# Expert outputs summed in memory by accumulating indirect DMA, instead of by rank and on VectorE at the end

## What is computed

```
idx, w = top-8 experts of 64 for each token, with weights
routed[t] = sum over the 8 experts e of token t:  w[t,e] * swiglu(h[t], w_gate[e], w_up[e], w_down[e])
shared[t] = swiglu(h[t], w_sh_gate, w_sh_up, w_sh_down)
f = routed + shared
y = x1 + g2 * rms_norm(f) * norm_post_ffn
```

## Time and profile before

| | |
|---|---|
| median of three runs | 1228.45 us (1228.25 to 1231.38) |
| the profiled execution, its own time | 1229.39 us |
| span of that execution (first to last instruction) | 1227.6 us |
| busy: PE, DVE, ACT, POOL | 1108.3, 902.1, 638.6, 186.9 us |
| mean granted TensorE clock | 0.944 of full speed |
| scatters, first and last issue | 545.1 and 1168.3 us |

### The profile page before, as it was taken

One profiled execution on the slowest core, in us unless ns is written; L12 is line 12 of the kernel. 1 busy time (PEld: TensorE's weight loads), 2 busy tenths in 40 slices (PEclk: granted clock), 3 DMA queues, 4 the chain that ended last, 5 costly groups with the idle time before them and its releaser, 6 DMA issues.

```text
span 1227.6 us, 18502 instructions
## 1 busy us (share of the span) xinstructions
PE 1108.3 (90%) x6006; PEld 804.5 (66%) x6006; DVE 902.1 (73%) x1306; ACT 638.6 (52%) x765; POOL 186.9 (15%) x185
## 2 busy tenths in 40 slices
PE   5899999999989989899999999999999999999700
PEld 0699999966444454467777777777777777777400
DVE  0732444267866776688899999988998888898878
ACT  1432222232421132357788777777777777777401
POOL 0200000000110010122222222222222222221102
PEclk8699999999879999999999999999999999999855
DMA  9532221163975124599999999999999999998996
GB/s 369 180 94 93 78 78 65 57 193 103 369 264 191 43 80 178 192 327 386 391 391 383 388 383 387 384 384 385 380 380 376 377 380 379 378 381 310 350 351 216
DMA packets 87140, 339.86 MB, mean 277 GB/s; under 512 B 12515, under 2 KB 36083, under 8 KB 59204
## 3 DMA queue, kind: packets, MB, share of 16 engines
q1 hardware_dynamic: 70724, 301.68, 66.6%
q0 software_dynamic: 16384, 37.78, 8.8%
HBM read 317.52 MB, written 42.86 MB: 294 GB/s over the span
## 4 chain that ended last, share of the span: by engine, by line
PE 41%; DMA 37%; DVE 14%; ACT 6%; issue 2%; SPq 1%; DVEq 0%; POOL 0%; POOLq 0%; ACTq 0%
DMA arena<-in_w_exp_down 31%; PE ps L1787 12%; DVE down_lo L1617 5%; PE ps L2023 4%; ACT down_hi L1102 4%; DMA arena<-in_w_ada 3%; PE ps L2215 3%; PE ps L2194 2%; PE ps L1780 2%; PE ps L2195 2%; PE ps L2196 2%; PE ps L2061 1%; DMA arena<-expert_rows 1%; PE ps L2198 1%; DMA arena<-in_w_in 1%
## 5 line engine op out<-in xcount | busy, mean ns | idle before, releaser
L1622 DVE TENSOR_TENSOR gu_lo<-w_gu,gu_hi 128x2048 fp32r<-128x2048 f32 (+1 forms) x128 | 258.5, 2020 | 6.0 <-ACT gu_hi L1096 1.1
L1096 ACT ACTIVATE gu_hi<-w_gu 128x2048 fp32r<-128x2048 f32 (+1 forms) x128 | 217.9, 1703 | 0.0
L1617 DVE TENSOR_TENSOR down_lo<-arena,down_hi 128x2048 fp32r<-128x2048 f32 x64 | 146.7, 2292 | 60.2 <-ACT down_hi L1102 60.2
L2194 PE MATMUL ps<-gu_hi,xT_hi 128*112 128x512 f32 x448 | 181.5, 405 | 3.7 <-DVE xT_lo L1627 2.6
L2195 PE MATMUL ps<-gu_lo,xT_hi 128*112 128x512 f32 x448 | 176.5, 394 | 0.0
L2196 PE MATMUL ps<-gu_hi,xT_lo 128*112 128x512 f32 x448 | 176.1, 393 | 0.0
L1102 ACT ACTIVATE down_hi<-arena 128x2048 fp32r<-128x2048 f32 x64 | 122.7, 1917 | 68.8 <-DMA arena<-in_w_exp_down 64.4
L811 POOL DMA_INDIRECT expert_rows<-arena,row_idx x64 | 69.8, 1091 | 360.7 <-ACT arena L1141 345.3
L1787 PE MATMUL ps<-w_hi,hT_hi 128*128 128x300 f32 x384 | 116.4, 303 | 2.0 <-DVE w_lo L1185 2.0
L1787 PE MATMUL ps<-w_lo,hT_hi 128*128 128x300 f32 x384 | 115.9, 302 | 0.0
L1787 PE MATMUL ps<-w_hi,hT_lo 128*128 128x300 f32 x384 | 115.7, 301 | 0.0
(11 more groups left out here) (297 smaller groups left out, 1891.5 us busy)
## 6 DMA issues: line engine op xcount, KB each, us to landing
w_gu<-in_w_exp_gate SPq DMA_DIRECT2D x64, 1024.0 KB
w_gu<-in_w_exp_up SPq DMA_DIRECT2D x64, 1024.0 KB
arena<-in_w_exp_down SPq DMA_DIRECT2D x64, 1024.0 KB
arena<-in_w_ada SPq DMA_DIRECT2D x24, 1024.0 KB, 8.8
arena<-in_w_in SPq DMA_DIRECT2D x12, 1200.0 KB, 5.6
arena<-expert_rows SPq DMA_DIRECT2D x9, 1024.0 KB, 13.8
arena<-expert_rows SPq DMA_DIRECT2D x4, 2048.0 KB, 13.0
arena<-in_x_prompt SPq DMA_DIRECT2D x8, 512.0 KB, 9.3
```

The costliest lines, as they stand in the source:

```text
L1096: a.activation(gu_hi[b % RING][:, :, ks], w_gu[b % U][:, :, ks], ACT.Copy).then_inc(s_ghi, 1)
L1617: v.tensor_tensor(down_lo[:, :, :], w_dn[b % RING], down_hi[:, :, :].bitcast(F32), ALU.subtract).then_inc(s_dlo, 1)
L1622: v.tensor_tensor(gu_lo[b % U][:, :, ks], w_gu[b % U][:, :, ks], gu_hi[b % RING][:, :, ks].bitcast(F32), ALU.subtract).then_inc(s_glo, 1)
L2194: pe.matmul(out, x_hi, gu_hi[r][:, :, k], start=(k == 0), stop=False)
```

## The change

`expert_rows` has one row for each token instead of eight, and begins as the shared expert's output: SP stores `shared` to it where it stored it to `kept_rows` before. Each scatter adds its rows to what is there (`compute_op=ALU.add`), and goes to the token's row. POOL waits, ahead of the first scatter, until that store is done. The other scatters wait for the one before them, as they did. At the end the summed rows are read back once, 4 KiB for each token, all five tiles behind the last scatter (`s_tick`); `x1` is loaded ahead of that, once the last block's gate and up matmuls are done. `low_ranks`, `middle_ranks` and `high_ranks` are gone, and with them `s_add` and the rank loads.

```diff
             def scatter(j, b):
                 g.wait_ge(s_ya, j + 2)
                 g.sem_inc(s_pulse, 1)
                 g.indirect_dma_start(expert_rows[:, :], bass.IndirectOffsetOnAxis(row_idx[0:T, b:b + 1].bitcast(U32), 0),
-                                     y_rows[0:T, b % 2], None, bounds_check=last_scatter,
-                                     oob_is_err=False).then_inc(s_ys[b], 16)
+                                     y_rows[0:T, b % 2], None, bounds_check=last_gather,
+                                     oob_is_err=False, compute_op=ALU.add).then_inc(s_ys[b], 16)
...
                     elif not is_first:
                         g.wait_ge(s_ys[U - 1], 16 * i)
+                    else:
+                        g.wait_ge(s_mst, 32 + 64)
...
-            for rows, buf in kept(N, shared):
-                sp.dma_start(rows, buf).then_inc(s_mst, 16)
+            sp.dma_start(expert_rows[0:SEQ, :].rearrange("(t p) d -> p t d", p=P), shared[:, 0:PT]).then_inc(s_mst, 16)
+            sp.dma_start(expert_rows[SEQ:N, :], shared[0:NS, PT]).then_inc(s_mst, 16)
...
             load_down(last * U + RING, RING, True)
-            sp.wait_ge(s_free, last * U + 2)
-            for t in range(2):
-                sp.wait_ge(s_gu, last * U + (t + 1))
-                rank_rows(ranks_low[t], 0, 4, t)
             load_down(last * U + 3, 3, True)
-            for t in range(2, NT):
-                ...
-                rank_rows(ranks_low[t], 0, 4, t)
             sp.wait_ge(s_gu, last * U + 4)
-            for rows, buf in kept(N, shared):
-                sp.dma_start(buf, rows).then_inc(s_bcg, 16)
-            sp.wait_ge(s_free, last * U + 4)
-            sp.wait_ge(s_dlo, last * U + 3)
+            for rows, buf in kept:
+                sp.dma_start(buf, rows).then_inc(s_fx, 16)
+            sp.wait_ge(s_tick, 1)
             for t in LAST_ORDER:
-                sp.wait_ge(s_add, (5, 4, 3, 4, 5)[t])
-                rank_rows(ranks_mid[t], 4, 2, t)
-            sp.wait_ge(s_y, last * U + U)
-            sp.wait_ge(s_tick, 1)
-            for n, t in enumerate(LAST_ORDER):
-                sp.wait_ge(s_add, NT + n + 1)
-                rank_rows(ranks_high[t], 6, 2, t)
-                ...
+                sp.dma_start(shared[0:ROWS[t], t], expert_rows[t * P:t * P + ROWS[t], :]).then_inc(s_yb[t], 16)
...
-                a.wait_ge(s_add, 2 * NT + n + 1)
-                a.activation(sq2[0:R], ranks_high[t][0:R, 0], ACT.Square, accum_out=ss[0:R, 3, t:t + 1]).then_inc(s_q3, 1)
+                a.wait_ge(s_yb[t], 16)
+                a.activation(sq2[0:R], shared[0:R, t], ACT.Square, accum_out=ss[0:R, 3, t:t + 1]).then_inc(s_q3, 1)
...
-                v.scalar_tensor_tensor(out=row_idx[0:T, b:b + 1], in0=slot_info_kept[0:T, bass.ds(at + 2, 1)], scalar=float(N),
-                                       in1=token_idx[0:T, b:b + 1], op0=ALU.mult, op1=ALU.add).then_inc(s_wt, 1)
+                v.tensor_copy(row_idx[0:T, b:b + 1], token_idx[0:T, b:b + 1]).then_inc(s_wt, 1)
...
             for n, t in enumerate(LAST_ORDER):
-                middle_ranks(t, NT + n + 1)
-            high_ranks(0, LAST_ORDER[0])
-            for n, t in enumerate(LAST_ORDER):
-                if n + 1 < NT:
-                    high_ranks(n + 1, LAST_ORDER[n + 1])
                 normalised(n, t)
```

More of the change, by code:

```diff
@@ L346, in hybrid_step @@
         slot_w = sb("slot_w", [P, U])
[L348 to L352, removed]
         sq2 = region(WORK0 + 8 * D, D)
@@ L493, in hybrid_step @@
         s_rowtile = sem("row_tile_changed")
-        s_yb = [sem(f"rank_rows_in{t}") for t in range(NT)]
-        s_add = sem("combined")
+        s_yb = [sem(f"summed_rows_in{t}") for t in range(NT)]
         s_q3 = sem("ffn_square_sum")
@@ L670, in _ @@
                 store_h2(t)
-            def kept(first, buf):
-                yield kept_rows[first:first + SEQ, :].rearrange("(t p) d -> p t d", p=P), buf[:, 0:PT]
-                yield kept_rows[first + SEQ:first + N, :], buf[0:NS, PT]
+            kept = ((kept_rows[0:SEQ, :].rearrange("(t p) d -> p t d", p=P), x1[:, 0:PT]), (kept_rows[SEQ:N, :], x1[0:NS, PT]))
             def load_gate_up(j, b, wait):
@@ L694, in load_down @@
                 sp.dma_start(w_dn[b % RING], down).then_inc(s_wdn[b % RING], 16)
-            for rows, buf in kept(0, x1):
+            for rows, buf in kept:
                 sp.dma_start(rows, buf).then_inc(s_mst, 16)
@@ L721, in _ @@
                     load_down(i * U + (b + RING), (b + RING) % U, True)
-            by_rank = expert_rows.rearrange("(k n) d -> n k d", n=N)
-            def rank_rows(to, first, k, t):
-                sp.dma_start(to[0:ROWS[t], 0:k], by_rank[t * P:t * P + ROWS[t], first:first + k]).then_inc(s_yb[t], 16)
             load_down(last * U + RING, RING, True)
-            sp.wait_ge(s_free, last * U + 2)
-            for t in range(2):
-                sp.wait_ge(s_gu, last * U + (t + 1))
-                rank_rows(ranks_low[t], 0, 4, t)
             load_down(last * U + 3, 3, True)
-            for t in range(2, NT):
[L734 to L737, removed]
-                rank_rows(ranks_low[t], 0, 4, t)
             sp.wait_ge(s_gu, last * U + 4)
-            for rows, buf in kept(N, shared):
-                sp.dma_start(buf, rows).then_inc(s_bcg, 16)
-            sp.wait_ge(s_free, last * U + 4)
-            sp.wait_ge(s_dlo, last * U + 3)
+            for rows, buf in kept:
+                sp.dma_start(buf, rows).then_inc(s_fx, 16)
+            sp.wait_ge(s_tick, 1)
             for t in LAST_ORDER:
-                sp.wait_ge(s_add, (5, 4, 3, 4, 5)[t])
-                rank_rows(ranks_mid[t], 4, 2, t)
-            sp.wait_ge(s_y, last * U + U)
-            sp.wait_ge(s_tick, 1)
-            for n, t in enumerate(LAST_ORDER):
-                sp.wait_ge(s_add, NT + n + 1)
-                rank_rows(ranks_high[t], 6, 2, t)
-                if n == 1:
-                    for rows, buf in kept(0, x1):
-                        sp.dma_start(buf, rows).then_inc(s_fx, 16)
+                sp.dma_start(shared[0:ROWS[t], t], expert_rows[t * P:t * P + ROWS[t], :]).then_inc(s_yb[t], 16)
             for n, t in enumerate(LAST_ORDER):
                 sp.wait_ge(s_fin, n + 1)
-                sp.dma_start(tok_rows(y_prompt, y_sample, t), ranks_high[t][0:ROWS[t], 1]).then_inc(s_out, 16)
+                sp.dma_start(tok_rows(y_prompt, y_sample, t), shared[0:ROWS[t], t]).then_inc(s_out, 16)
             sp.wait_ge(s_out, 16 * (3 * H + NT))
@@ L796, in _ @@
             last_gather = g.to_reg(N - 1)
-            last_scatter = g.to_reg(N * TOPK - 1)
             def gather(j, b, wait=True):
@@ L1671, in turn @@
                         gate_up_low(i * U + (b + 3), b + 3, 0)
[L1672 to L1693, removed]
             def normalised(n, t):
-                R, y = ROWS[t], ranks_high[t][0:ROWS[t]]
+                R, y = ROWS[t], shared[0:ROWS[t], t]
                 v.wait_ge(s_r3, n + 1)
-                step(v.scalar_tensor_tensor(out=y[:, 1], in0=y[:, 0], scalar=rstd[0:R, 3, t:t + 1], in1=bcg2[t // PT][0:R],
+                step(v.scalar_tensor_tensor(out=y, in0=y, scalar=rstd[0:R, 3, t:t + 1], in1=bcg2[t // PT][0:R],
                                             op0=ALU.mult, op1=ALU.mult))
-                v.wait_ge(s_fx, 32)
-                mark(v.tensor_tensor(y[:, 1], y[:, 1], x1[0:R, t], ALU.add), s_fin, n + 1)
+                mark(v.tensor_tensor(y, y, x1[0:R, t], ALU.add), s_fin, n + 1)
             last = last_turn(v)
@@ L1706, in _ @@
             turn(last, True)
-            v.wait_ge(s_bcg, 16 * (SB + 1 + SB + 2))
+            v.wait_ge(s_bcg, 16 * (SB + 1 + SB))
+            v.wait_ge(s_fx, 32)
             for n, t in enumerate(LAST_ORDER):
-                middle_ranks(t, NT + n + 1)
-            high_ranks(0, LAST_ORDER[0])
-            for n, t in enumerate(LAST_ORDER):
-                if n + 1 < NT:
-                    high_ranks(n + 1, LAST_ORDER[n + 1])
                 normalised(n, t)
@@ L2278 @@
     args.append(nc.dram_tensor("h2_rows", (N, D), F32, kind="Internal").ap())
-    args.append(nc.dram_tensor("expert_rows", (N * TOPK, D), F32, kind="Internal").ap())
-    args.append(nc.dram_tensor("kept_rows", (2 * N, D), F32, kind="Internal").ap())
+    args.append(nc.dram_tensor("expert_rows", (N, D), F32, kind="Internal").ap())
+    args.append(nc.dram_tensor("kept_rows", (N, D), F32, kind="Internal").ap())
     hybrid_step(nc, *args)
```

## The result

The changed kernel takes 1239.8 us, median of 6 runs, beside 1229.7 for the kernel before on the same chip: a ratio of 1.0078, with an interval of 1.0056 to 1.0099, so it is 7 to 12 us slower. The forecast was 1239. The profiled execution spans 1237.1 us, 9.5 more than before.

The account below looks back on a forecast made before the run. The prediction took PE and the DMA transfers to bound the block loop together. 41 us more for the adds less 30 at the end is +11, 1240 us profiled, so 1239 as median; range 1194 to 1280.

Parts of the forecast that it names:

- What bounds the kernel: Block loop: PE's 9.78 and DMA's 9.75 us a block lie within 0.1 us, so PE hides no added transfers.
- The accumulate: one more pass: Block loop: each scatter also fetches the rows it adds to, 0.70 us a block over 59 blocks, 41 us more.
- One scatter at a time: POOL's wait between scatters: landing 8.7 us, at most 10.1, against a period of 10.5; POOL still waits for ACT.
- D: Rival, block loop: scatter landing over 10.5 us sets the period; with 12 us, +96 us, 1325 us; chance 0.12.
- A: The forecast, block loop: one more pass, paid by the loop; -10 to +24 us, 1218 to 1252; chance 0.52.
- The last three blocks and the end: Last landing moves from 1176.3 to about 1175, then 22.8 us without rank loads and sums: 30 us less.
- The indices: DVE copies token indices instead of a multiply and add, once a block: same count and size, nothing.
- B: Rival, block loop: the fetch is hidden beside the loads, period stays 9.87 us; 1198 us; chance 0.21.
- C: Rival, block loop: an added row costs two more passes or more; +53 us, 1281 us; chance 0.15.

Follow-up runs that it names:

- The new gather: Gather's transfer spread over all 128 partitions instead of 112, in the kernel before: 1223.2 us, 6.0 less; the same edit in the changed kernel: 1206.1 us.

## Why the prediction was right

*What bounds the kernel.* Right, and the step on which all hangs: PE at 9.78 and the transfers at 9.75 us a block, nothing hidden. The new gather confirms it from the other side: with less to do for the DMA engines PE is busy 559 of 560 us.

*The accumulate: one more pass.* Right. Forecast 0.70 us a block within 0.41 to 0.85, 41 us. Queue 0 took 51.6 us more, 0.81 a block; the loop grew by 39.5 us from the first scatter to the last; the add alone costs 39.7 by the medians and 43.5 by the profiled executions, half of the adds about half of it. By plain rows in its place the period is 10.63 for 10.65 us. By ACT's writes the period grew by 0.73 us and all 59 periods to the 60th block pay, 42.9 us. Behind them the adds cost the loop nothing, as said: ACT's last four periods are 35.2 us with them and 35.7 with plain scatters. Only the last landing is longer, 5.2 us for 3.3.

By the Trainium skill, Collectives: The Full Stack, section "The bandwidth ceiling: the fold count and why AG ≠ RS ≠ AR", a reduce in the DMA path reads two sources where a copy reads one. That page speaks of collectives; the estimate worked out from its rates was 44 us, 0.74 us a block. The runs agree with it, with 40 to 44 us and 0.81 us a block of queue 0.

*One scatter at a time.* Half wrong. The landing was put at 8.7 us and is 9.3; "POOL still waits for ACT and not for the landing" is wrong in 27 of 53 blocks. By its own list of signs ("if POOL waits for the landing (D)") the forecast would have been wrong, but the sign does not tell D from A: POOL may wait for a landing while nobody waits for POOL. That the landing would not set the period was right: without those waits the period is 10.57 us, and ACT never sat idle for POOL. A missing term is that POOL's own part of the scatter, which the landing includes, takes 1.61 us for 1.09. And the longest landing was put at 10.1 us, 0.4 under the new period, and up to 11.1 were measured. (Where this part says "the first rival below", it means D, the fourth.) The margin was as thin as said: two plain transfers in a row, or a landing of 10.4 us, make this wait the limit and cost 50 to 64 us.

*The last three blocks and the end.* Forecast: landing at 1175 + 41 = 1216, 22.8 us more to the end, 30 us less in all. Measured: 1214.7, 22.4, and 29.6 by the kernel with plain scatters. That the last landing came out within 2 us is luck in part: 1.5 us less in the last block and 41 us more in the loop would have put ACT's last write at 1203.0, and it is at 1206.2; the last scatter, at a DMA share of 0.44, lands in 5.2 us and not 7.9. Behind it the first tile's load takes 3.6 us from its issue, for 3.8 with the issue; square sum and root take 2.2 us and not 3.1, DVE's stretch 13.3 and not 12.8. (The 4.5 us on the chain are the second tile's load.)

*The indices.* Nothing, as said: with them and plain scatters the scatters' period is that of before, 9.87 us.

*The rivals.* B is out: its 1198 us is what the kernel without the add takes. C is out by the size of the add. D is a neighbour: not this kernel's limit, but that of both kernels with two scatters in a row and of the one with the wider scatter, where ACT waits for POOL.

Where the gain went: 18.9 MB of ranks that are no longer read back are 18.9 MB that the adds fetch. The change moves them from the end, where they and DVE's sums cost some 30 us, into a loop that has no room for them, where they cost some 40.

## What to carry to other kernels

Count an accumulating transfer as two passes of its rows, also where the profile's bytes show one, and ask whether the stretch that it runs in has room: the same adds cost nothing in the last four blocks here and full price in the 59 before them. A transfer that must wait for the one before it has a second limit, its landing: compare landing and period. Do not stop at the engine that issues it: that POOL waited for a landing meant nothing (27 and 50 blocks) while ACT did not wait for POOL, and 50 to 64 us where it did, with the DMA share down at 0.95. And when a loop is short of transfer rate, try the layout of its small transfers; here a gather's was worth 33 us in the changed kernel, three times what the change itself cost.

## What the hardware showed that was not expected

- An indirect gather to 112 partitions costs the DMA engines more than one to 128 in which 16 more slots are skipped: at the same share of 1.02 they move 385 GB/s with the first and 404 with the second, fetches of the adds counted, and the period of ACT's writes is 10.60 and 10.07 us. With it the kernel before takes both queues some 10 us less for the same bytes. The Trainium skill, SBUF — State Buffer, section "Door 1: The DMA port swizzle (why `[64,N]` ≈ `[32,N]`)", has each DMA engine serve a port of its own in a transfer over 128 partitions; it says nothing of one over 112. That engines meet at ports when 112 are dealt out would be in keeping with it, but no run shows a port, and the cause is open.
- The same widening of the accumulating scatter made its landing 10.4 us for 9.1 and the kernel 64 us slower.
- POOL is busy 1.61 us (median) with an accumulating scatter in the changed kernel, up to 3.56, and 1.09 with a plain one in its place. The add is not all of it: the median was 1.50 with the wider gather, and a plain scatter issued right behind another took 2.73 us in one kernel and 0.93 in another. What it depends on is open.
- Two plain scatters of a block one behind the other, both waited for, made a period of 11.69 us in the kernel before; with the wait one block further back it is 10.63. The bytes are the same.
